# A two-layer hybrid trunk on one core: the last output chunk as a job of its own, new x chunk by chunk, rotary rows swapped by DMA

## The chip, the cores and the metric

The kernel runs as one program on one core of a Trainium2 chip. The metric is the device time of an execution in microseconds (us). The engines are TensorE (PE: matmul; PEld: its weight loads), VectorE (DVE), ScalarE (ACT), GpSimd (POOL) and SyncE (SP), which here only issues DMAs.

## The reference, cut to what matters

Two layers over x of 256 tokens by 1024 channels, all float32. Each layer:

```python
u = _rms_norm(x, pre_mix_norm_w[l])
proj = u @ w_in[l]
qkv_a, z_a, a_a, b_a, cq, ckv, k_rope, gate_logits = _split_cols(proj, PROJ_SIZES)
...
q_b = (_rms_norm(cq, q_a_norm_w[l]) @ w_uq[l]).reshape(b, s, MLA_HEADS, MLA_QK_DIM)
q_b = jnp.concatenate([q_b[..., :MLA_NOPE], _rope(q_b[..., MLA_NOPE:], cos[:, :, None, :], sin[:, :, None, :])], axis=-1)
k_pe = jnp.broadcast_to(_rope(k_rope, cos, sin)[:, :, None, :], (b, s, MLA_HEADS, MLA_ROPE))
y_b = _chunk_causal_attention(q_b, k_b, v_b) @ w_branch_b[l]
h = gates[:, :, 0] * y_a + gates[:, :, 1] * y_b
x = x + _rms_norm(h @ w_out[l], post_mix_norm_w[l])
u = _rms_norm(x, pre_ffn_norm_w[l])
f = jnp.square(jax.nn.relu(u @ w_ff1[l])) @ w_ff2[l]
x = x + _rms_norm(f, post_ffn_norm_w[l])
```

Left out is branch A: short convolution, SiLU, the chunked gated delta rule and a per-head norm, giving y_a. `_rope` turns the two 32-wide halves of a 64-wide rotary part: x1·cos − x2·sin, x2·cos + x1·sin.

## The kernel before

x stays in SBUF, channels on partitions: `xT` is 8 chunks of 128 channels by 256 tokens. Every weight is cut into pieces of 128 x 1024 (152 a layer), fetched by SP in order into a ring of four (`raw`). ScalarE rounds a piece to `whi` (`split_hi`, L973), VectorE makes the rest `wlo` (`split_lo`, L1296). The moving side is split the same way, so each 128x128 weight block costs three products of 256 columns: whi·high (L559), whi·low (L560), wlo·high (L561), in `chunk_products`.

The work is a list of jobs (`JOBS`), each 256 output channels wide into one of three PSUM banks `dense`; a job over 1024 input channels has two pieces and 48 products, a `uq` job one piece, an `ff2` job eight. `schedule()` writes one order (`ORDER`) of jobs and small steps by hand, and every engine walks it with its own part of each step. `splits_wanted` says how far ahead of each step the pieces are split; ScalarE waits there for the piece four back to be released by its products (`steps_done`).

A layer's four borders matter here. "out" (4 jobs) is followed by `ysum`, `post`, `fsplit_x` and then "ff1" (16 jobs); "ff2" (4 jobs) by `ysum`, `post` and the next layer's "lat" jobs (ckv, cq, and one with k_rope) or the end. At such a border ScalarE squares the last job's output (L1095), TensorE adds the squares over channels by products with a matrix of ones (`ysum`, L955: four float32 products of 256 columns), ScalarE takes the inverse root (L984, L986), and `post` on VectorE and GpSimd multiplies `yT` by it (L1618) and adds to `xT` (L1623, and L1733 on GpSimd for chunk pairs 1 and 3). ScalarE then scales and rounds each chunk (`fuh` L1037 or `xh` L1003), VectorE makes the low part (`ful` L1632 or `xl` L1303), and the first job goes chunk by chunk, waiting for the low part.

The "lat" jobs use unnormalised x, so they can run before the norm of x. After the first two of them TensorE adds the squares of x (`norm`, L664), ScalarE takes the root, VectorE and ScalarE make `utmp`, `uh`, `ul`, which the "k" job's first half uses; its second half waits for a piece whose split stands behind these steps.

Rotary: TensorE multiplies by a permutation matrix (`perm`) to swap the 32-row halves of the key (`kr_`, L737) and of two groups of queries (`qrope`, L903); VectorE multiplies by cos and sin and adds. The attention units 0 to 5 run between "gate" jobs (`sc`, `tr`, `pv`; probabilities times values is L945).

Of the kernel before, what the change touches and what calls it, by code (L numbers as in the profile page):

```python
# [23 lines left out]
P = 128  # L24
# [12 lines left out]
PI_BELOW = 3.1415925  # L37
RING = 4
# [17 lines left out]
C_ID, C_UT, C_NEG, C_M1, C_IQ, C_LV, C_ONE, C_PERM, C_AM, C_FREQ = 0, 128, 256, 384, 416, 448, 512, 640, 768, 1024  # L56
# [4 lines left out]
def jobs_of_a_layer():  # L61


    jobs, n = [], 0
    for kind, numbers, pieces in (("lat", range(3), 2), ("k", range(1), 2), ("z", range(1), 2), ("k", range(1, 4), 2),
# [4 lines left out]
                                  ("out", range(4), 2), ("ff1", range(16), 2), ("ff2", range(4), 8)):  # L70
        for i in numbers:
            jobs.append((kind, i, list(range(int(n), max(int(n) + 1, int(n + pieces))))))
            n += pieces
    return jobs, int(n)
# [12 lines left out]
def steps_through(n, job=False):  # L87


    if job:  # L90
        return sum(len(p) for _, _, p in JOBS[:n + 1])
    if n < 0:
        return n + 1
    return sum(len([q for q in p if q <= n]) for _, _, p in JOBS)


NSTEP = steps_through(NJOB - 1, job=True)
# [8 lines left out]
def schedule():  # L106

    o = [("xsplit", 0), ("xsplit", 1), ("sq", 0), ("sq", 1), ("sqsum", 0), ("sq", 2), ("sq", 3), ("sqsum", 1)]
# [113 lines left out]
    for i in range(4):  # L222
        job("out", i)
        if i in (1, 2):
            o.append(("yadd", i - 1))
    o += [("ysum", 0), ("post", 0), ("fsplit_x", 0)]
    for i in range(16):
        o.append(("job", JOB["ff1", i]))
        if i == 0:
            o.append(("squares", 1))  # L230
        if i == 1:
            o.append(("norm", 1))
        flush()
        late.append(("fsplit", i))
    flush()
    for i in range(4):
        job("ff2", i)
        if i in (1, 2):
            o.append(("yadd", 1 + i))
    o += [("ysum", 1), ("post", 1)]  # L240
# [7 lines left out]
def build(nc, x_in, pos_in, w_in, prm_in, cst_in, out):  # L248
    with ExitStack() as ctx:
# [122 lines left out]
        perm = cst[:, C_PERM:C_PERM + P]  # L372
# [48 lines left out]
        x_by_pool, x_by_dve, y_add = (signal("x_by_pool", 4), signal("x_by_dve", 4), signal("y_add", 4))  # L421
# [12 lines left out]
        kr_mm, kr_b, kr_out, ktrans_mm = (signal("kr_mm", 1), signal("kr_b", 2), signal("kr_out", 2), signal("ktrans_mm", 2))  # L434
# [14 lines left out]
        on_hi, on_lo, qr_mm, qr_b = (signal("on_hi", 4), signal("on_lo", 4), signal("qr_mm", 2), signal("qr_b", 4))  # L449
# [4 lines left out]
        h_hi, h_lo, y_sq, y_mm = (signal("h_hi", 4), signal("h_lo", 4), signal("y_sq", 8), signal("y_mm", 2))  # L454
        y_r, y_scaled, f_sq = (signal("y_r", 4), signal("y_scaled", 8), signal("f_sq", 16))
        f_hi, f_lo = (signal("f_hi", 16), signal("f_lo", 16))

# [6 lines left out]
        def products_done(l, j):  # L464

            return l * NSTEP + steps_through(j, job=True) + RING

# [20 lines left out]
        def splits_wanted(l, what, n):  # L488

            if what == "job":  # L490
                ahead = 2 if n == NJOB - 1 else RING
                return min(l * NPIECE + JOBS[n][2][-1] + ahead, DEPTH * NPIECE)
            if what == "half":
                return l * NPIECE + JOBS[n][2][0] + RING
            return l * NPIECE + {("xsplit", 1): 1 + l, ("sq", 0): 2 + l, ("sqsum", 1): 3 + l}.get((what, n), 0)

        splits_at, seen = [], 0
        for l in range(DEPTH):
            for what, n in ORDER:
                goal = max(seen, splits_wanted(l, what, n))  # L500
                splits_at.append(range(seen, goal))
                seen = goal
        assert seen == DEPTH * NPIECE

        def steps_with_splits(l):
            return zip(ORDER, splits_at[l * len(ORDER):(l + 1) * len(ORDER)])
# [3 lines left out]
        def _(sp):  # L510
            def x_part(c):
                sp.dma_start(xT[:, 2 * c:2 * c + 2, :], x_in[:, 2 * c:2 * c + 2, :]).then_inc(s_x[c], 16)

            x_part(0)
            for n in range(DEPTH * NPIECE):
                sp.wait_ge(lo_ready, n + 1)
                sp.dma_start(raw[n % RING][:], w_in[n]).then_inc(loaded[n % RING], 16)
                if n == 0:
                    for c in range(1, 4):
                        x_part(c)  # L520
            for c in range(4):
                pair = slice(2 * c, 2 * c + 2)
                x_pair = x_by_pool if c % 2 else x_by_dve
                sp.wait_ge(x_pair, due(DEPTH, x_pair, 1 + c // 2))
# [5 lines left out]
        def _(pe):  # L530
# [16 lines left out]
            def chunk_products(bank, n, k0, kcount, cols, ahi, alo, first, last, total_k, need=None):  # L547

                h_, l_ = whi[n % RING], wlo[n % RING]
                nch = cols // P  # L550
                for k in range(kcount):
                    if need is not None:
                        need(k0 + k)
                    for c in range(nch):
                        ws = slice(k * cols + c * P, k * cols + (c + 1) * P)
                        o_ = bank[:, c * S:(c + 1) * S]
                        is_first = first and k == 0 and c == 0
                        is_last = last and k == kcount - 1 and c == nch - 1
# [3 lines left out]
                return x_  # L562

            def half(l, j):

                def need(k):
                    if j == JOB["k", 0] and k % 2 == 0:
                        pe.wait_ge(u_lo, due(l, u_lo, k // 2 + 1))
                banks_free(l, j)
                n = JOBS[j][2][0]  # L570
                piece(l, n)
                chunk_products(dense[j % 3], n, 0, 4, 256, uh, ul, True, False, KD, need).then_inc(steps_done, 1)

            def job(l, j):
                kind, i, pieces = JOBS[j]
                bank = dense[j % 3]
                begun = ("half", j) in ORDER
# [1304 lines left out]
```

## Time and profile before

| what | value |
| --- | --- |
| device time, median of 3 runs | 1077.89 us (1075.48 to 1079.14) |
| span of the profiled execution | 1064.2 us |
| median less that span | 13.7 us |
| TensorE busy | 1010.9 us (95%) |
| VectorE, ScalarE, GpSimd busy | 732.4, 557.7, 137.9 us |
| HBM read | 161.25 MB, 153 GB/s over the span |

The page gives the span of one execution, from its first to its last instruction; its device time is not listed apart from the runs', and what lies outside the span is the start and end of the program. Positions below are microseconds from the span's start. Busy time of TensorE includes time at the lower of its two clocks.

### The profile page before, as it was taken

To read this page: it belongs to the slowest core of one execution; us is meant where nothing else is said; L and a number is where in the kernel's file an instruction comes from. 1 tells how busy PE (TensorE), PEld (TensorE's weight loads), DVE (VectorE), ACT (ScalarE), POOL (GpSimd) and SP (SyncE) were. 2 spreads that over 40 slices of the span, in tenths; PEclk is the share of its full clock that TensorE was granted. 3 is DMA by queue.
4 is the path that set the end of the run, shared out by engine and by line. 5 is a ranking of instruction groups with operands and counts; after the bars stand their busy time and mean duration, and the time that the engine had idled before them with its cause. 6 is when DMAs were issued, how large, how long until landed. Compare 5 with 4: busy or idle time off the path is not lost.

```text
span 1064.2 us, 24113 instructions
## 1 busy us (share of the span) xinstructions
PE 1010.9 (95%) x10552; PEld 987.3 (93%) x10552; DVE 732.4 (69%) x982; ACT 557.7 (52%) x786; POOL 137.9 (13%) x109
## 2 busy tenths in 40 slices
PE   5899899999999899999978999999999989999996
PEld 5899889899999899999978998998999979999995
DVE  6886648698566698745388766677875777886453
ACT  6576365755444554443356753767454445444441
POOL 6201000230000322200010000014000013221001
PEclk9999999999999899999989999999999999999998
DMA  7344424334556176666534443334356544766661
GB/s 252 135 141 158 124 82 130 118 106 149 188 180 197 65 224 192 200 196 195 160 119 135 143 142 121 115 106 121 117 166 189 166 153 145 213 197 199 193 185 40
DMA packets 45608, 163.85 MB, mean 154 GB/s; under 512 B 5184, under 2 KB 5440, under 8 KB 45504
## 3 DMA queue, kind: packets, MB, share of 16 engines
q1 hardware_dynamic: 44928, 161.50, 48.2%
q8 instruction: 83, 1.36, 0.5%
q10 hardware_dynamic: 576, 0.82, 0.2%
q14 instruction: 21, 0.17, 0.0%
HBM read 161.25 MB, written 1.05 MB: 153 GB/s over the span
## 4 chain that ended last, share of the span: by engine, by line
PE 91%; DVE 5%; issue 2%; ACT 2%; DMA 1%; POOL 0%; POOLq 0%; SPq 0%; ACTq 0%; DVEq 0%
PE dense L559 25%; PE dense L560 25%; PE dense L561 24%; DVE wlo L1296 1%; PE sides L945 1%; PE sides L799 1%; PE sides L919 1%; PE sides L920 1%; PE sides L791 1%; DVE utmp L1332 1%; PE sides L955 1%; PE sides L759 1%; PE sides L769 1%; PE sides L895 1%; PE sides L718 1%
## 5 line engine op out<-in xcount | busy, mean ns | idle before, releaser
L1296 DVE TENSOR_TENSOR wlo<-raw,whi 128x1024 fp32r<-128x1024 f32 (+1 forms) x304 | 397.9, 1318 | 195.8 <-ACT whi L973 195.5
L973 ACT ACTIVATE whi<-raw 128x1024 fp32r<-128x1024 f32 (+1 forms) x304 | 315.6, 1047 | 225.7 <-PE dense L561 222.0
L559 PE MATMUL dense<-uh,whi 128*128 128x256 f32 x768 | 223.3, 291 | 5.3 <-DVE wlo L1296 5.3
L560 PE MATMUL dense<-ul,whi 128*128 128x256 f32 x768 | 216.3, 282 | 2.6 <-issue 2.6
L561 PE MATMUL dense<-uh,wlo 128*128 128x256 f32 x768 | 216.3, 282 | 0.0
L559 PEld LDWEIGHTS dense<-uh,whi 128*128 128x128 f32 x768 | 147.2, 192 | 7.8 <-DVE wlo L1296 5.7
L559 PE MATMUL dense<-fuh,whi 128*128 128x256 f32 x512 | 144.3, 282 | 9.9 <-DVE ful L1632 9.6
L561 PEld LDWEIGHTS dense<-uh,wlo 128*128 128x128 f32 x768 | 147.2, 192 | 1.6 <-issue 1.6
L560 PEld LDWEIGHTS dense<-ul,whi 128*128 128x128 f32 x768 | 146.7, 191 | 1.5 <-issue 1.3
L560 PE MATMUL dense<-ful,whi 128*128 128x256 f32 x512 | 143.5, 280 | 0.0
L561 PE MATMUL dense<-fuh,wlo 128*128 128x256 f32 x512 | 143.5, 280 | 0.0
L559 PE MATMUL dense<-fh,whi 128*128 128x256 f32 x512 | 141.3, 276 | 0.0
L560 PE MATMUL dense<-fl,whi 128*128 128x256 f32 x512 | 141.3, 276 | 0.0
L561 PE MATMUL dense<-fh,wlo 128*128 128x256 f32 x512 | 141.3, 276 | 0.0
L559 PEld LDWEIGHTS dense<-fuh,whi 128*128 128x128 f32 x512 | 98.3, 192 | 11.1 <-issue 10.3
L560 PEld LDWEIGHTS dense<-ful,whi 128*128 128x128 f32 x512 | 98.2, 192 | 0.1
L561 PEld LDWEIGHTS dense<-fuh,wlo 128*128 128x128 f32 x512 | 98.1, 192 | 0.0
L560 PEld LDWEIGHTS dense<-fl,whi 128*128 128x128 f32 x512 | 96.1, 188 | 0.0
L559 PEld LDWEIGHTS dense<-fh,whi 128*128 128x128 f32 x512 | 96.1, 188 | 0.0
L561 PEld LDWEIGHTS dense<-fh,wlo 128*128 128x128 f32 x512 | 96.1, 188 | 0.0
L1727 POOL TENSOR_TENSOR fr<-fr 128x512 f32<-128x512 f32 x32 | 46.5, 1453 | 119.3 <-DVE fr L1604 119.3
L1697 POOL TENSOR_TENSOR sq<-sq,sq 128x512 f32<-128x512 f32 x8 | 10.4, 1296 | 353.0 <-ACT sq L1095 353.0
(289 smaller groups left out, 1923.2 us busy)
## 6 DMA issues: line engine op xcount, KB each, us to landing
raw<-weights SPq DMA_DIRECT2D x304, 512.0 KB, 3.7
xT<-x_t SPq DMA_DIRECT2D x4, 256.0 KB, 5.7
out_t<-xT SPq DMA_DIRECT2D x4, 256.0 KB, 2.3
cst<-consts ACTq DMA_DIRECT2D x1, 512.0 KB, 6.5
prm_all<-params ACTq DMA_DIRECT2D x1, 150.0 KB, 4.0
pos_i<-pos ACTq DMA_DIRECT2D x1, 128.0 KB, 5.5
cst<-consts ACTq DMA_DIRECT2D x1, 6.0 KB, 5.8
```

Of the source, the lines that this page charges most:

```text
L559: mm(o_, h_[:, ws], ahi[:, k0 + k, :], start=is_first, stop=False, skip_group_check=True)
L560: mm(o_, h_[:, ws], alo[:, k0 + k, :], start=False, stop=False, skip_group_check=True)
L561: x_ = mm(o_, l_[:, ws], ahi[:, k0 + k, :], start=False, stop=is_last, skip_group_check=True)
L718: r = mm(side[KS_BANK[i // 2]][:, c:c + 1], k_squares[i][:, e * S + t * P:e * S + (t + 1) * P], ones[:, 0:1], start=True, stop=True)
L759: r = mm(side[KK_BANK[n]][:, e * P:(e + 1) * P], kT[:, h, ts_], kT[:, h, ts_], start=True, stop=True)
L769: r = mm(side[QK_BANK[n]][:, e * P:(e + 1) * P], kT[:, h, ts_], qT[:, h, ts_], start=True, stop=True)
L791: r = mm(side[e][rows, 16 * g:16 * (g + 1)], LT[rows, g, e, rows], evens(Xq[rows, e, g, :], SIZES[lv]), start=True, stop=True)
L799: r = mm(side[e][rows, 16 * g:16 * (g + 1)], XTq[rows, e, g, :], PBq[rows, e, g, 0:16], start=True, stop=True)
L895: mm(side[2 + i % 2][:], ones, sq[i % 2][:], start=True, stop=True).then_inc(on_mm, 1)
L973: return A(o_, i_, ACT.Copy)
L1296: TT(wlo[s][:, 0:w], raw[s][:, 0:w], f32(whi[s][:, 0:w]), ALU.subtract).then_inc(lo_ready, 1)
L1727: G(fr[i % 4][:], fr[i % 4][:], fr[i % 4][:], ALU.mult).then_inc(f_sq, 1)
```

## The change

1. **Last chunk.** "out" and "ff2" become five jobs: three of 256 channels, then one each for chunk 6 and chunk 7. For "out" both use the same two pieces (`held`); for "ff2" each has four pieces of its own, eight input chunks deep. `early_sums` adds the squares of chunks 0 to 6 (three float32 products) inside the last job; `ysum` keeps one product.
2. **New x by chunk.** `post` becomes the steps `times`, `add`, `high`, `low` over the groups chunk 0, chunk 1, and pairs (2,3), (4,5), (6,7). VectorE does groups 0 to 2, GpSimd both the multiply and the add of (4,5) and (6,7); at the very end VectorE does (4,5) too.
3. **Interleaved first jobs.** Jobs 0 and 1 of "lat" and of "ff1" run together (`pair_of_jobs`): for each x chunk the eight products with the high part once that is there, then, after the low part, the other four. Their pieces are laid out in turns. `ff1` 2's first half goes ahead of `norm` 1.
4. **Splits.** ScalarE and VectorE get tables of their own; pieces for the next stage are split inside the turn.
5. **Rotary.** The `perm` products are gone. SP copies the swapped rows SBUF to SBUF (`swap_key_rows`, `swap_query_rows`, two DMAs each, of 32 KB and 128 KB each), from its one queue of weight loads. The rotary columns are laid out anew; the key's zeroing and adding takes four memsets and four additions of 32 partitions on VectorE instead of two and two of 64.
6. **Probability product.** The very last of unit 5 is done as two products of 64 output rows.

```diff
-                                  ("out", range(4), 2), ("ff1", range(16), 2), ("ff2", range(4), 8)):
+                                  ("out", range(4), 2), ("ff1", range(16), 2), ("ff2", range(3), 8), ("ff2", (3, 4), 4)):
...
+            if kind in PAIRED and i < 2:
+                mine = [int(n) - i, int(n) - i + 2]
...
+        if kind == "out":
+            jobs.append((kind, 4, mine))
...
+NEW_X = [[0], [1], [2, 3], [4, 5], [6, 7]]
+def by_dve(l, w):
+    return 4 if (l, w) == (DEPTH - 1, 1) else 3
...
+    def turn(w):
+        o.extend([("ysum", w), ("post", w)])
+        step = lambda what, g: o.append((what, 5 * w + g))
+        for g in range(2):
+            for what in ("times", "add", "high"):
+                step(what, g)
+        step("low", 0)
+        step("times", 2)
+        step("low", 1)
+        step("add", 2)
+        step("high", 2)
+        for g in (3, 4):
+            for what in ("times", "add", "high"):
+                step(what, g)
+        for g in (2, 3, 4):
+            step("low", g)
...
+    turn(0)
+    o.append(("squares", 1))
     for i in range(16):
+        if i == 2:
+            half("ff1", 2)
+            o.append(("norm", 1))
+            late.extend([("fsplit", 0), ("fsplit", 1)])
...
+            behind = JOBS[JOB["ff2" if n >= 5 else "out", 4]][2][-1] + RING + 1
+            if engine == "act":
+                if what == "high":
+                    return min(base + behind + {0: 0, 4: 1, 5: 0}.get(n, -1), DEPTH * NPIECE)
+                if l:
+                    return base + {("xsplit", 0): 4, ("xsplit", 2): 5, ("sq", 0): 6}.get((what, n), 0)
+            if engine == "dve" and what == "low":
+                return min(base + behind + {3: 0, 4: 1}.get(n % 5, -1), DEPTH * NPIECE)
+            if l:
+                return base + {("xsplit", 2): 6}.get((what, n), 0)
+            return {("xsplit", 1): 1, ("sq", 0): 2, ("sqsum", 1): 3}.get((what, n), 0)
...
+                if p == JOBS[JOB["kn", 0]][2][0] + 6:
+                    swap_key_rows(l)
+                for i in range(2):
+                    if p == JOBS[JOB["uq", 4 + i]][2][0] + 7:
+                        swap_query_rows(l, i)
...
+            def swap_query_rows(l, i):
+                sp.wait_ge(t_oo, due(l, t_oo, 2))
+                sp.wait_ge(act_evac, l * NACT_EVAC + evacs_through(JOB["uq", 4 + i])[1])
+                rotary = qr[:, 2 * i:2 * i + 2, :].rearrange("p c s -> p (c s)")
+                sp.dma_start(E[i][0:ROPE, :], rotary[ROPE:P]).then_inc(qr_swapped[i], 16)
+                sp.dma_start(E[i][ROPE:P, :], rotary[0:ROPE]).then_inc(qr_swapped[i], 16)
...
+            def pair_of_jobs(l, j):
...
+                for k in range(KD):
+                    h_, e = divmod(k, 4)
+                    places = [slice(e * 256 + c * P, e * 256 + (c + 1) * P) for c in range(2)]
+                    pe.wait_ge(high, due(l, high, k + 1))
+                    for jj in both:
+                        n = JOBS[jj][2][h_]
+                        wh, wl = piece(l, n)
+                        for c, ws in enumerate(places):
+                            o_ = dense[jj % 3][:, c * S:(c + 1) * S]
+                            mm(o_, wh[:, ws], a_[:, k, :], start=(k == 0 and c == 0), stop=False, skip_group_check=True)
+                            mm(o_, wl[:, ws], a_[:, k, :], start=False, stop=False, skip_group_check=True)
+                    pe.wait_ge(low, due(l, low, k + 1))
+                    for jj in both:
+                        wh = whi[JOBS[jj][2][h_] % RING]
+                        for c, ws in enumerate(places):
+                            r = mm(dense[jj % 3][:, c * S:(c + 1) * S], wh[:, ws], b_[:, k, :], start=False,
+                                   stop=(k == KD - 1 and c == 1), skip_group_check=True)
+                        if e == 3:
+                            r.then_inc(steps_done, 1)
...
-            def kr_(l, _):
-                pe.wait_ge(vtrans_out, due(l, vtrans_out, 4))
-                mm(side[4][0:64, 0:S], perm[0:64, 0:64], krx[0:64, :], start=True, stop=True).then_inc(kr_mm, 1)
...
-            def qrope(l, i):
-                mm(side[4][:], perm, qr[:, 2 * i:2 * i + 2, :], start=True, stop=True).then_inc(qr_mm, 1)
...
+                        if n == 5 and h == hs[-1] and kt == qt:
+                            for d in (slice(0, 64), slice(64, P)):
+                                r = mm(o_[d], vt[:, kt, h, d], p_, start=False, stop=True)
...
+            def early_sums(l, w):
+                pe.wait_ge(y_add, due(l, y_add, 2 * w + 2))
+                for e in range(2):
+                    mm(side[1][:, 0:S], ones, sq[0][:, e * S:(e + 1) * S], start=(e == 0), stop=False)
+                pe.wait_ge(y_sq, due(l, y_sq, 5 * w + 4))
+                mm(side[1][:, 0:S], ones, sq[1][:, 0:S], start=False, stop=False)
```

## Rows read from the trace of the kernel before

**Rows 1.** The page, first part: busy time of the engines.
```profile
PE 1010.9 (95%) x10552; PEld 987.3 (93%) x10552; DVE 732.4 (69%) x982; ACT 557.7 (52%) x786; POOL 137.9 (13%) x109
```

**Rows 2.** What TensorE waited for: us in total, times, longest us.
```profile
PE dense L559 <- DVE wlo L1296: 19.2, 5, 11.2
```

**Rows 3.** Timeline of TensorE: start, us, instruction [idle before, who ended it].
```profile
38.01 0.39 PE L559 MATMUL dense<-uh,whi 128*128 128x256 f32 x1 [3.86 <-DVE wlo L1296]
...
349.96 0.55 PE L559 MATMUL dense<-fuh,whi 128*128 128x256 f32 x1 [4.78 <-DVE ful L1632]
```

**Rows 4.** Busy time by window; PEclk 1.00 is 2.4 GHz, 0.50 is 1.2 GHz.
```profile
11.20:14.30 3.10, 3.10 (x14) 3.10 (x15) 3.10 (x6) 3.10 (x7) 2.85 (x4) 1.00 0.99 375
...
350.20:355.40 5.20, 5.20 (x25) 5.20 (x26) 4.80 (x9) 2.09 (x6) 1.45 (x1) 0.50 0.01 3
360.00:529.00 169.00, 168.79 (x1480) 168.38 (x1480) 107.80 (x98) 73.56 (x81) 26.99 (x19) 1.00 0.61 192
```

**Rows 5.** Chain that ended last at layer 1's border out to ff1: start, us.
```profile
343.37 1.83 PE sides L955 x8
...
346.18 0.70 DVE yT L1618
...
364.11 1.74 PE sides L664 x8
```

**Rows 6.** The same chain at the border of the layers, and at the end.
```profile
529.55 1.83 PE sides L955 x8
...
553.23 0.88 PE sides L664 x4
...
1052.42 1.83 PE sides L955 x8
```

**Rows 7.** Timelines of GpSimd and VectorE in the ff1 stage.
```profile
394.36 1.42 POOL L1727 TENSOR_TENSOR fr<-fr 128x512 f32<-128x512 f32 x1 [4.02 <-DVE fr L1604]
394.80 2.06 DVE L1296 TENSOR_TENSOR wlo<-raw,whi 128x1024 fp32r<-128x1024 f32 x1
```

**Rows 8.** Groups by line: x count | busy us, mean ns | idle before.
```profile
L1618 DVE TENSOR_TENSOR yT<-yT,rn 128x512 f32<-128x512 f32 x16 | 10.9, 684 | 4.8 <-ACT rn L986 4.8
...
L973 ACT ACTIVATE whi<-raw 128x1024 fp32r<-128x1024 f32 (+1 forms) x304 | 315.6, 1047 | 225.7 <-PE dense L561 222.0
```

**Rows 9.** Timeline of ScalarE: squares of 512 and of 256 columns.
```profile
343.40 0.60 ACT L1095 ACTIVATE sq<-dense 128x512 f32<-128x512 f32 x1 [1.71 <-PE dense L561]
...
564.37 0.36 ACT L1075 ACTIVATE sq_q<-dense 128x256 f32<-128x256 f32 x1
```

**Rows 10.** The chain, layer 1: rotary key, rotary queries, probabilities times values.
```profile
184.28 0.57 PE sides L737 x2
...
204.57 0.86 PE sides L903 x2
...
274.63 0.89 PE sides L945 x8
```

**Rows 11.** DMA issues (KB each, us to landing), and the first use of the rotary key.
```profile
out_t<-xT SPq DMA_DIRECT2D x4, 256.0 KB, 2.3
cst<-consts ACTq DMA_DIRECT2D x1, 6.0 KB, 5.8
...
L920 PE MATMUL sides<-krz,qr x64: 275/328/380, 218.1 to 779.1; 128*128 128x128 f32 x32, 128*128 128x256 f32 x32
```

**Rows 12.** The start: VectorE's second split, the norm's root in both layers, TensorE.
```profile
14.33 1.22 DVE L1296 TENSOR_TENSOR wlo<-raw,whi 128x1024 fp32r<-128x1024 f32 x1
...
25.15 0.48 ACT rn L1021
...
554.13 0.48 ACT rn L1021
...
564.83 0.39 PE L559 MATMUL dense<-uh,whi 128*128 128x256 f32 x1 [1.40 <-DVE wlo L1296]
```

**Rows 13.** Timeline of GpSimd: the last addition.
```profile
1060.20 1.26 POOL L1733 TENSOR_TENSOR xT<-xT,yT 128x512 f32<-128x512 f32 x1 [1.23 <-DVE yT L1618]
```

More of the change, by code:

```diff
@@ L37 @@
 PI_BELOW = 3.1415925
+PAIRED = ("lat", "ff1")
 RING = 4
@@ L82, with steps_of_a_layer, steps_through, steps_of_job @@
 NDVE_EVAC = NJOB - NACT_EVAC
[L87 to L97, printed above, removed]
+def steps_of_a_layer():
+    steps = []
+    for j, (kind, i, pieces) in enumerate(JOBS):
+        if kind in PAIRED and i == 0:
+            steps += [(j + e, JOBS[j + e][2][h_]) for h_ in range(2) for e in range(2)]
+        elif not (kind in PAIRED and i == 1):
+            steps += [(j, n) for n in pieces]
+    return steps
+STEPS = steps_of_a_layer()
+def steps_through(n):
+    return n + 1 if n < 0 else 1 + max(k for k, (_, piece) in enumerate(STEPS) if piece <= n)
+def steps_of_job(j):
+    return 1 + max(k for k, (job, _) in enumerate(STEPS) if job == j)
+NSTEP = len(STEPS)
+def chunks_of(kind, i):
+    return (2 * i, 2 * i + 1) if i < 3 else (i + 3,)
+NEW_X = [[0], [1], [2, 3], [4, 5], [6, 7]]
+def by_dve(l, w):
+    return 4 if (l, w) == (DEPTH - 1, 1) else 3
 def evacs_through(j):
@@ L239, in schedule @@
             o.append(("yadd", 1 + i))
[L240 removed]
+    turn(1)
     return o
@@ L484, in piece_width, with splits_wanted @@
             return KQ * 256 if kind == "uq" else PIECE
-        def splits_wanted(l, what, n):
+        def splits_wanted(l, what, n, engine):
+            base = l * NPIECE
             if what == "job":
-                ahead = 2 if n == NJOB - 1 else RING
-                return min(l * NPIECE + JOBS[n][2][-1] + ahead, DEPTH * NPIECE)
+                kind, i, pieces = JOBS[n]
+                held = kind == "out" and i == 3
+                return min(base + pieces[0 if held else -1] + RING, DEPTH * NPIECE)
@@ L493, in splits_wanted @@
             if what == "half":
[L494 to L506, printed above, removed]
+                return base + JOBS[n][2][0] + RING
@@ L1274, in _ @@
             for l in range(DEPTH):
-                for (what, n), pieces in steps_with_splits(l):
+                for (what, n), pieces in steps_with_splits(l, act_splits):
                     for p_ in pieces:
@@ L1307, in xsplit @@
                 if l == 0:
-                    for e in (range(2), range(2, KD))[part]:
+                    for e in (range(2), range(2, 6), range(6, KD))[part]:
                         x_low(l, e)
@@ L1664, in _ @@
             for l in range(DEPTH):
-                for (what, n), pieces in steps_with_splits(l):
+                for (what, n), pieces in steps_with_splits(l, dve_splits):
                     for p_ in pieces:
@@ L1819, in wide, with in_turns @@
                 pieces.append(blocks(w, 4 * h_, 4, cols))
+        def in_turns(w, first, second):
+            for h_ in range(2):
+                for cols in (first, second):
+                    pieces.append(blocks(w, 4 * h_, 4, cols))
         krope = kr0 + r(ROPE)
```

301 lines of the change are left out of this document (176 added, 125 removed).

## The prediction, made before the changed kernel had run

> **What bounds the kernel now.** I read the page first: TensorE is busy for 1010.9 of the 1064.2 us [rows 1]. Then its waits [rows 2] and its timeline [rows 3]: it hardly waits except at the start, where x or u are renewed, and at the end. So there are two ways to win: fewer products, or shorter borders. The windows show a second cost of a border: after the 4.78 us wait at 349.96 the products run at a granted clock of 0.50, 25 in 5.2 us or 0.21 us each; in the long stretch behind they run at 1.00, 1480 in 169 us, 0.114 us each [rows 4]. Last I read the chain at each border, because it gives a border's whole length, waits and slow clock together: from the sums of squares (343.37) to the end of the first two ff1 jobs (364.11) 20.7 us; between the layers (529.55 to 553.23) 23.7 us; at the end (1052.42 to 1064.2) 11.8 us [rows 5, 6]. The two jobs are 96 products, about 11 us, so each border costs some 10 to 12 us beyond its work.
>
> **Rotary and the halved product.** Over both layers two key products of 0.57 us and four query products of 0.86 us go [rows 10]: 1.14 + 3.44 = 4.6 us. Their lines stand in the chain, so all of it counts. Four probability products take 0.89 us, so one is 0.22 us; cutting it in two adds between 0 (each half takes half) and 0.22 us a layer; I take 0.1, so +0.2. Sum −4.4. The copies are hidden if they land in time. The queries are in SBUF soon after 204.57, where the old product read them, and are first used at 218.1 [rows 10, 11]: 13.5 us. The second group comes one job of 18 products and two sums later, some 4 us, which leaves 9.5, of which VectorE's three steps of 0.68 [rows 8] need 2. No row shows a copy from SBUF to SBUF. Nearest are the output writes of 256 KB, 2.3 us, and a first small load, 5.8 us [rows 11]; both fit. I take 2.3. Ahead of both copies SP waits for an evacuation; behind it stand only weight loads, with four pieces in the ring, at 18 products each (2.1 us) some 8 us, so a stall of 1 to 2 us is covered. VectorE's two more memsets and two more additions per layer, at most four one-chunk operations, 1.7 us, lie under products: it is busy 69% [rows 1]. Without the cover each late microsecond would stop TensorE in both layers.
>
> **A border, first half: up to the inverse root.** Today it takes 2.8 us from the sums to the first multiply (343.37 to 346.18) [rows 5]. The last square shrinks from 0.60 to 0.36 us [rows 9], and one product of ones, 0.43 us (a quarter of the 1.74 at 364.11), stands behind it instead of two: 2.15 us. But the three early sums now stand in the stream of products: +1.3 us, where before two of the four ran under the square. So this half is a loss of 0.6 us at each of four borders; it pays only through one-chunk multiplies.
>
> **A border, second half: the port.** In the ff1 stage a wlo took 2.06 us beside a GpSimd operation (1.42, which itself first waits for VectorE), against 1.22 at 14.33 [rows 7, 12]. So each GpSimd operation holds VectorE up by about 0.85 us, and the change has four at a border for two. The Trainium skill ("SBUF — State Buffer", "SBUF: two separate sides") says the two engines' shared port pair is an exclusive lock, held for the whole instruction; by it each hold would be GpSimd's whole 1.3 us [rows 13], four times 0.45 or 1.8 us more a border; the trace agrees that there is a hold, and shows it at 0.84.
>
> *out to ff1.* A VectorE operation takes 0.68 us for 512 columns and 1.22 for 1024 [rows 8, 12], so for the 256 of one chunk I take 0.42. After the root it does two multiplies, two additions and two low parts of one chunk (2.5), then multiply and addition of a pair (1.3), beside four holds (3.4): 7.2 us. ScalarE's high part of chunk 2 adds 0.5. The first two chunks' 24 products lie inside; 72 are left, at 0.115 us 8.3. Sum 2.15 + 1.3 + 7.2 + 0.5 + 8.3 = 19.4 against 20.7. For the clock I add 0.5: 0 if the shorter waits keep it up, 1.5 if it falls and some 15 products run at 0.21 [rows 4]: −0.8, twice −1.6. Bounds for the pair: −7 with no holds, +4 with holds of 1.3 and a low clock.
>
> *Between the layers.* The second norm needs VectorE's list finished: after the root twelve one-chunk operations (5.0), a pair twice (1.3), three splits (1.15 each, 3.4), three sums of squares (2.0), four holds (3.4), plus 2.5 waiting for ScalarE and for the fourth chunk's products to free the ring. 17.6 + 2.15 + 1.3 = 21.0 against 23.7: −2.7. Bounds −6 and 0.
>
> **The start is a border too, and it gets worse.** The pair needs pieces 0 and 1 at its first chunk. Piece 1's wlo begins at 14.33 and ends at 15.55 [rows 12]; nothing in the diff makes that sooner. Now TensorE fills that time with piece 0, from 11.2 us on [rows 2]; then it does four products and stops. The remaining 92 take 10.5 us at full clock: 26.1. Today's first products run at the slow pace, 14 in 3.1 us, though that column shows 1.00 [rows 4]; these will too, after a longer idle: 20 of them at 0.1 us more, +2, so 28.1 against 24.25 (the root at 25.15 [rows 12] less the 0.9 seen between 553.23 and 554.13): +3.9. Further, both jobs now end together, so before the root ScalarE does two squares and a split between (0.6 + 1.05 + 0.6) [rows 8, 9], 2.3 us where the sums of squares of x take 0.9: 1.3 us more. Against that, GpSimd works on the angle tables during this stretch: root to k's second half is 12.9 us (25.15 to 38.01) in layer 1 and 10.7 (554.13 to 564.83) in layer 2 [rows 3, 12]; shifted later, I give back 2.2. Sum +3.0. Bounds +1 and +5.
>
> **The end.** VectorE: four one-chunk operations (1.7), four of a pair (2.7), two holds (1.7): 6.1, with 2.15 and 1.3 9.5 us to the last addition, where today GpSimd ends at 1061.46, 9.0 us after 1052.42 [rows 6, 13]. Two writes then go out back to back: between 0 and the 2.3 us of one landing [rows 11], I take 0.4. Sum +0.9. Bounds −0.5 and +1.5.
>
> **Sum.** −4.4 − 1.6 − 2.7 + 3.0 + 0.9 = −4.8 us on the span of 1064.2: 1059.4. The median of the runs stands 13.7 above that span, and I leave that alone: 1077.9 − 4.8 = 1073.1 us.
>
> **The rivals.**
> - *Faster than that (24%):* the borders gain what they are laid out for. For it: 10 to 12 us of each border are not products, and the first eight products no longer wait for a low part. Against it: the port. If GpSimd's operations hold VectorE up half as long, each border gains 1.7 more and the start loses 1 less: −4.8 − 6.8 − 1.0, about 1065.5.
> - *The borders cancel the rotary gain (19%):* if the port is held longer (1.2 us a hold) and the granted clock falls in ff1, the two ff1 borders give nothing back and the layer border 1: −4.4 + 0 − 1 + 4 + 1.2, about 1077.7.
> - *Slower (13%), the port alone:* if GpSimd's two-step groups win the port each time VectorE's addition waits for its multiply, chunk 0 is new only after two holds, and the chain by chunk has become a chain by GpSimd operation. The price is four holds of 1.3 us [rows 13] a border, 1.8 us more at each of four, plus 1.5 of slow clock at two: −4.8 + 7.2 + 3 = +5.4, 1083. It decides from about 1.2 us more a border than I count. Against it: wlo at 394.80 was held 0.84 us, not 1.3. The page of the Trainium skill named above states the longer hold.
> - *The copies are late (4%):* if the second query copy takes over 8 us, the scores wait. At 12 us it costs 4 a layer: 1081.
>
> **How the numbers follow.** The likeliest case, 40%, is 1073.1; its own range is 1070 to 1076.5. A measurement of this kernel can tell 0.3%, 3.2 us, from no change, so faster means below 1074.7. That takes the first rival (24%) and three quarters of the likeliest (30%) and a little of the second: 0.55. Same (1074.7 to 1081.1): a quarter of the likeliest (10%), nearly all of the second (18%) and the milder of the slower ones (3%): 0.31. Slower: 0.14. The range 1065 to 1080 leaves out the far half of the fastest and most of the slower rival.
>
> **What would show it.** Right: no rows L737 and L903; TensorE's chain from early sums to the end of the first pair 0.5 to 1.5 us shorter at ff1 and 2 to 3.5 at the layers' border; VectorE's one-chunk addition taking over 1 us beside GpSimd; a new wait of some 3.5 us at the start between the fourth and fifth dense product, ended by wlo; the norm's root in layer 1 at 28 to 31 instead of 25.15; the last addition by VectorE. Wrong: a wait ahead of L920 (copies), or products on the second chunk starting within 5 us of the root (no port), or a first pair held at 0.50 clock for more than 4 us.

## The result and the profile after

The changed kernel takes 1081.27 us (median of 20 runs, 1074.32 to 1090.03), the kernel before, beside it on the same chips, 1073.54 us (20 runs, 1066.20 to 1082.18). The ratio is 1.0091, 95% interval 1.0071 to 1.0112: slower by 0.9%, some 9.8 us (the two medians lie 7.7 us apart), where I had forecast 4.8 us less. The ratios here and below go by the fast executions; left out by them are, among others, one of d_best at 1688.88 us and one of d_ropes at 1518.16. The profiled execution of the changed kernel has a span of 1083.9 us and a device time of 1085.66. So only 1.8 us lie outside the span; the 13.7 us that I left between span and median were for the greater part spread between executions. The two profiled spans are 19.7 us apart, two to two and a half times the distance of the runs, and one pair of profiles must not be read as if it were the median.

The page, first part, changed kernel. TensorE's busy time rose by 10.2 us with eight instructions fewer [rows 1]:

```profile
PE 1021.1 (94%) x10544; PEld 997.4 (92%) x10544; DVE 737.2 (68%) x992; ACT 558.5 (52%) x790; POOL 148.3 (14%) x115
```

What TensorE waited for (us in total, times, longest), changed kernel:

```profile
PE dense L680 <- ACT fuh L1168: 7.3, 2, 3.6
...
PE dense L659 <- DVE wlo L1429: 4.7, 4, 2.6
PE sides L1063 <- DVE E L1695: 4.3, 2, 2.2
PE dense L680 <- DVE wlo L1429: 3.1, 1, 3.1
PE dense L686 <- DVE ful L1783: 2.9, 2, 1.4
```

L680 to L686 are the paired jobs, L659 to L661 the other dense products (L559 to L561 before). The wait of 3.1 us at the fifth product is the one that I had announced. At each ff1 border 3.6 and 1.4 stand for the 4.78 of [rows 3]. The third row answers to nothing before: TensorE stops 2.2 us a layer ahead of the transposes of the first probabilities.

**Rotary.** The chain of the changed kernel from the second query group's issue to those transposes (start, us):

```profile
205.17 0.52 SPq L606
205.72 4.20 DMA E<-qr
209.95 0.69 DVE E L1587
...
211.96 1.70 DVE oT L1670
213.66 0.87 DVE wlo L1429
214.53 1.69 DVE E L1587
...
228.69 0.70 DVE E L1695
229.44 0.86 PE sides L1063 x4
```

and its DMA issues (KB each, us to landing):

```profile
E<-qr SPq DMA_DIRECT2D x8, 128.0 KB, 4.4
...
krb<-krx SPq DMA_DIRECT2D x4, 32.0 KB, 3.1
```

The first copy lands at 209.9, and VectorE, which stood waiting for it (3.18 us idle by its timeline), starts the rotary step there; the same step began at 205.79 before. TensorE does not need the queries until 217.8. But VectorE walks one written list: the norm of branch A (`oT`), three splits and the first softmax stand behind that step, each 3 to 5 us later than before (1.05 of it was there ahead of the stage), and the gaps down to 228.69 take up only about 1 us of that. The lateness comes out at the softmax. How long the stage is can be read between two marks on TensorE, the first products of L991 (L851 before) and the first probabilities times values, L1081 (L945). The kernel before, then the changed one:

```profile
160.79 1.95 PE L851 MATMUL sides<-vtok,XT 128*128 128x128 f32 x16
...
234.76 1.05 PE L945 MATMUL sides<-PT,vt 128*128 128x128 f32 x8
```

```profile
161.84 1.39 PE L991 MATMUL sides<-vtok,XT 128*128 128x128 f32 x11
...
238.80 1.05 PE L1081 MATMUL sides<-PT,vt 128*128 128x128 f32 x8
```

73.97 against 76.96 us: 3.0 longer, though three perm products (2.3 us) are gone. Layer 2 says the same, 73.96 against 76.90.

The wait of 2.16 us is only a part of that; the other is the clock behind it. The transposes and the eight products of the next scores take 3.7 us in the changed kernel (229.44 to 233.15) and 2.0 us before (227.14 to 229.11), 1.7 us more. The same stretch in the changed kernel and in d_ropes (an experiment below, with a wait of 2.31 us at the same place), columns as under "The pace":

```profile
229.40:233.00 3.60, 3.56 (x11) 0.55 0.06 9
```

```profile
230.40:234.00 3.60, 3.53 (x24) 1.00 0.04 6
```

In d_ropes the clock stayed up and they took 2.0 us (230.47 to 232.50). The layer of a_whole in which it stayed up has 75.69 us between the two marks, the one in which it fell 77.55. So a wait of this length did not always bring the clock down here; where it did, wait and slow clock together cost 3.9 us for 2.16 of wait.

**The port.** Timeline of VectorE and GpSimd behind the root at the out to ff1 border, changed kernel:

```profile
348.72 0.43 DVE L1761 TENSOR_TENSOR yT<-yT,rn 128x256 f32<-128x256 f32 x1 [1.15 <-ACT rn L1116]
348.76 1.51 POOL L1877 TENSOR_TENSOR yT<-yT,rn 128x512 f32<-128x512 f32 x1 [6.99 <-ACT rn L1116]
349.18 1.37 DVE L1770 TENSOR_TENSOR xT<-xT,yT 128x256 f32<-128x256 f32 x1
350.35 1.33 POOL L1886 TENSOR_TENSOR xT<-xT,yT 128x512 f32<-128x512 f32 x1
350.47 1.48 DVE L1761 TENSOR_TENSOR yT<-yT,rn 128x256 f32<-128x256 f32 x1
...
351.99 1.38 DVE L1770 TENSOR_TENSOR xT<-xT,yT 128x256 f32<-128x256 f32 x1
...
353.30 1.48 DVE L1783 SCALAR_TENSOR_TENSOR ful<-xT,prm_all,fuh 128x256 fp32r<-128x256 f32 x1
```

One-chunk operations take 0.42 or 0.48 us alone. Each of the four behind the first takes 1.37 to 1.48: four holds of 0.95 to 1.06 us, all on the chain from the root to chunk 1. GpSimd's four operations stand back to back from the root on, and each goes beside one of VectorE's. Four holds were in the forecast as in the slower rival; their size lies between the two (0.85 and 1.3), and chunk 0 is new after one hold, not after two as the rival had it. Each of the four held operations ends 0.27 to 0.29 us after the end of GpSimd's operation beside it: the hold is what was left of that one when VectorE's began, 0.12 to 0.42 us behind it. The page "SBUF — State Buffer" of the Trainium skill ("SBUF: two separate sides") calls the shared port pair an exclusive lock held for the whole instruction; the trace agrees, as far as GpSimd's times can be trusted.

**The pace.** Windows of TensorE in long stretches of dense products; columns are window, length, busy (count), granted clock, DMA share, GB/s. The first window lies in `ya`/`yb`, the second in ff1. Kernel before, then changed kernel:

```profile
285.00:315.00 30.00, 30.00 (x257) 1.00 0.60 185
380.00:420.00 40.00, 40.00 (x355) 1.00 0.68 209
```

```profile
285.00:315.00 30.00, 30.00 (x267) 1.00 0.69 206
380.00:420.00 40.00, 40.00 (x342) 1.00 0.67 202
```

At the same granted clock of 1.00 there are two spacings: 30/267 and 40/355 us a product, and 30/257 and 40/342. A window also counts the products that only reach into it, so these quotients are a little low; from start to start the timelines give 0.1133 and 0.1178 us. The change swapped them: the 564 products of `ya`, `yb` (the outputs of the two branches) and `out` got 2.5 us a layer shorter, the 1392 of the ff1 and ff2 stretch 6.3 us a layer longer. I had read 0.114 as the price of a product and left it alone.

### The profile page after: what moved, and what is told of

Its sections match the earlier page's. It is cut to its first block, busy times and chain, and to the rows that moved or that the text cites. A ratio compares the mean times of both kernels' runs of the same rounds, so it can differ in the third digit from the quotient of the medians.

```text
span 1083.9 us, 24184 instructions
## 1 busy us (share of the span) xinstructions
PE 1021.1 (94%) x10544; PEld 997.4 (92%) x10544; DVE 737.2 (68%) x992; ACT 558.5 (52%) x790; POOL 148.3 (14%) x115
## 3 DMA queue, kind: packets, MB, share of 16 engines
HBM read 161.18 MB, written 1.05 MB: 150 GB/s over the span
## 4 chain that ended last, share of the span: by engine, by line
PE 84%; DVE 9%; issue 3%; ACT 2%; DMA 1%; SPq 0%; ACTq 0%; DVEq 0%
PE dense L659 23%; PE dense L660 22%; PE dense L661 22%; DVE wlo L1429 2%; PE dense L686 2%; PE dense L680 1%; PE dense L681 1%; DVE oT L1670 1%; PE sides L939 1%; PE sides L1081 1%; PE sides L931 1%; ACT whi L1103 1%; DVE yT L1761 1%; DMA E<-qr 1%; PE sides L1051 1%
## 5 line engine op out<-in xcount | busy, mean ns | idle before, releaser
L1429 DVE TENSOR_TENSOR wlo<-raw,whi 128x1024 fp32r<-128x1024 f32 (+1 forms) x304 | 393.3, 1302 | 214.8 <-ACT whi L1103 214.5
L659 PE MATMUL dense<-uh,whi 128*128 128x256 f32 x768 | 222.5, 290 | 4.3 <-DVE wlo L1429 4.3
L661 PE MATMUL dense<-uh,wlo 128*128 128x256 f32 x768 | 215.0, 280 | 0.0
L659 PEld LDWEIGHTS dense<-uh,whi 128*128 128x128 f32 x768 | 146.4, 191 | 6.9 <-DVE wlo L1429 4.9
L661 PEld LDWEIGHTS dense<-uh,wlo 128*128 128x128 f32 x768 | 145.7, 190 | 0.2 <-issue 0.2
L659 PE MATMUL dense<-fh,whi 128*128 128x256 f32 x512 | 144.2, 282 | 0.0
L660 PE MATMUL dense<-fl,whi 128*128 128x256 f32 x512 | 143.8, 281 | 0.0
L661 PE MATMUL dense<-fh,wlo 128*128 128x256 f32 x512 | 143.8, 281 | 0.0
L659 PE MATMUL dense<-fuh,whi 128*128 128x256 f32 x448 | 126.3, 282 | 0.4 <-DVE wlo L1429 0.4
L660 PE MATMUL dense<-ful,whi 128*128 128x256 f32 x448 | 125.8, 281 | 0.0
L661 PE MATMUL dense<-fuh,wlo 128*128 128x256 f32 x448 | 125.8, 281 | 0.0
L659 PEld LDWEIGHTS dense<-fh,whi 128*128 128x128 f32 x512 | 98.2, 192 | 0.1
L661 PEld LDWEIGHTS dense<-fh,wlo 128*128 128x128 f32 x512 | 96.1, 188 | 0.0
L659 PEld LDWEIGHTS dense<-fuh,whi 128*128 128x128 f32 x448 | 85.9, 192 | 0.8 <-issue 0.8
L660 PEld LDWEIGHTS dense<-ful,whi 128*128 128x128 f32 x448 | 84.2, 188 | 0.1
L661 PEld LDWEIGHTS dense<-fuh,wlo 128*128 128x128 f32 x448 | 84.1, 188 | 0.0
```

Of the source, the lines that this page charges most:

```text
L659: mm(o_, h_[:, ws], ahi[:, k0 + k, :], start=is_first, stop=False, skip_group_check=True)
L660: mm(o_, h_[:, ws], alo[:, k0 + k, :], start=False, stop=False, skip_group_check=True)
L661: x_ = mm(o_, l_[:, ws], ahi[:, k0 + k, :], start=False, stop=is_last, skip_group_check=True)
L1429: TT(wlo[s][:, 0:w], raw[s][:, 0:w], f32(whi[s][:, 0:w]), ALU.subtract).then_inc(lo_ready, 1)
```

## The experiments

All of these kernels compute the whole reference. Ratios are to the kernel before, run beside them on the same chip; 0.01 is 10.7 us. Line numbers are each kernel's own.

**Can one small product turn the pace?** a_sum5 and b_sum5 are the changed kernel and the one before with the last norm product ahead of the stretch split by columns; a_whole takes the halved probability product out of the change, b_half puts it alone into the kernel before.

```diff
# a_sum5, b_sum5
-                    r = mm(side[0][:, 0:S], ones, q_[:, c, :], ...)
+                    if w and c == 5:
+                        mm(side[0][:, 0:P], ones, q_[:, c, 0:P], start=False, stop=False, ...)
+                        r = mm(side[0][:, P:S], ones, q_[:, c, P:S], start=False, stop=True, ...)
...
# b_half (a_whole: the reverse)
+                        if n == 5 and h == hs[-1] and kt == qt:
+                            for d in (slice(0, 64), slice(64, P)):
+                                r = mm(o_[d], vt[:, kt, h, d], p_, start=False, stop=True)
...
```

> The changed kernel, with the last of the four norm products ahead of ff1's job 2 (L808) done as two of 128 columns instead of one of 256; nothing else. Pace theory: the products of a long stretch start either 0.113 or 0.118 us apart at the same full clock, and which of the two is settled by the small products between two stretches; one small product more turns it. Then the 1392 products behind that sum, which take 0.118 us each in the changed kernel, take 0.113: 6.3 us less a layer, some 12 us less in all, and the kernel is about as fast as before or faster (1068 to 1072). Rival, borders: the 7 us a layer were lost to VectorE and GpSimd at the borders; one product more changes the time by under 1 us and the windows behind it show 0.118 as before.

> The kernel before, with the last of the four norm products (L664) in two of 128 columns. Pace theory: the 1440 products behind it turn from 0.113 to 0.118 us, 6.5 us more a layer, some 13 us more in all. Rival: the same time within 0.5 us.

> The changed kernel with the last probability product whole again, as before the change. Pace theory: the 564 products of ya, yb and out, 0.113 us apart in the changed kernel, go back to 0.118 (2.5 us more a layer); if the pace is only handed on, the ff stage behind turns as well, to 0.113 (6.3 us less a layer), together 7 to 8 us less. Rival, borders: the same time within 0.5 us, the half product being worth 0.1.

> The kernel before, with only the last probability product halved. Pace theory: ya, yb and out turn from 0.118 to 0.113 us (2.5 us less a layer); the 1440 products of ff1 and ff2 turn from 0.113 to 0.118 if the pace is handed on (6.5 us more a layer), together about 8 us more; if it is not handed on, 5 us less. Rival: the same time within 0.5 us.

Measured: a_sum5 1.0101 (1.0054 to 1.0149) and b_sum5 0.9979 (0.9952 to 1.0006), and neither turned a stretch: my rule "one small product more turns it" fell. b_half gives 0.9925 (0.9892 to 0.9958), 8 us less, a_whole 1.0130 (1.0075 to 1.0186), 4 us above the changed kernel but with overlapping intervals. The window of b_half's profile that answers to the first one above:

```profile
285.00:315.00 30.00, 30.00 (x267) 1.00 0.62 186
```

So the halved product, which I priced at 0.1 us a layer of loss, wins by itself; of the six parts only this one and the rotary were tried alone. Its stretch accounts for 5 of the 8 us. The profile of a_whole does not mirror this cleanly: its `ya`/`yb`/`out` stretch has the short spacing in layer 1 and the long one in layer 2, and its ff stretches, long in the changed kernel, are short in both layers, though its median is no better.

**Rotary alone, and where VectorE waits.** b_rot is the kernel before with part 5 only. The next kernels move VectorE's two rotary steps in the written list.

```diff
# a_late (on the change), b_hrl (kernel before + halved product + copies)
-        if i >= 4:
-            late.append(("qrope", i - 4))
+        if n in (1, 2):
+            late.append(("qrope", n - 1))
# d_ropes (on a_dve below)
+        if n == 1:
+            late.extend([("qrope", 0), ("qrope", 1)])
```

> The kernel before with only part 5 of the change: rotary rows swapped by SP's copies, no perm products. My prediction's step: 4.6 us less over both layers, the copies hidden. Theory from the trace of after: the first query copy lands at 209.6, VectorE stands still for 3.2 us waiting for it (209.95), everything behind it in VectorE's list (norm of the branch, splits, the first softmax) is 3 us late, and the first transposes wait 2.2 us more: from the vtok products to the probability products 2.9 us a layer longer than before instead of 2.2 shorter, so 4 to 6 us slower in all. If instead the loss belongs to other parts of the change, this kernel is 4 us faster than before.

> The changed kernel with VectorE's two rotary steps (qrope) each one uq job later in the written order, behind the branch's norm steps; copies and everything else as in the change. Theory: VectorE does not stand still for the first copy, the wait for the softmax (2.2 us a layer ahead of the first transposes) goes, 2 to 3 us less a layer, 4 to 6 in all. Rival: VectorE's list is simply too full there (memsets, additions and held operations), and the order changes nothing: same within 1 us.

> The kernel before with the halved probability product, the rotary by copies, and VectorE's rotary steps one uq job later. If the copies are hidden this way, it has the 4.6 us of the perm products on top of what the halved product alone gave (ratio 0.9925): about 0.988 to 0.989. If the copies still cost, it is slower than the halved product alone.

> The kernel with the new x all on VectorE (a_dve), and both rotary steps of VectorE behind the first of the branch's norm steps and its split, ahead of the second: late enough for the first copy, early enough for the scores, where putting each one job later made the scores wait 2.16 us for the second. Theory: neither the wait ahead of the scores nor the one ahead of the transposes, so vtok to the first probabilities times values takes 71 to 73 us against 77; 3 to 5 us a layer less than a_dve's. Rival: VectorE's list is too full in any order, and about 2 us of wait stay at one of the two places.

b_rot: 1.0024 (0.9994 to 1.0054). The 0.9957 that my 4.6 us less would have been is outside. Its trace (of one of its longer executions, 1079.68 us) has the wait ahead of the transposes in both layers (2.37 and 2.36 us). a_late: 1.0106 (1.0078 to 1.0134), no gain: that wait went and this one came in its place, since the scores need both groups:

```profile
217.70 0.46 PE L1051 MATMUL sides<-kn,qn 128*128 128x128 f32 x2 [2.16 <-DVE qr L1590]
```

b_hrl: 1.0004 (0.9976 to 1.0031), with the same wait; the copies ate the 8 us that the halved product had brought. d_ropes: 0.9971 (0.9933 to 1.0010), 4 us under its own base a_dve, the intervals overlapping; the wait ahead of the scores is gone, the other is not:

```profile
230.47 0.66 PE L1063 MATMUL sides<-cst,E 128*128 128x128 f32 x4 [2.31 <-DVE E L1695]
```

Its rival holds for the wait: in three orders some 2.2 us come out at one place or the other. But the stage takes 74.49 and 74.54 us between the marks, where a_dve has 77.83 and 76.67; the theory had hoped for 71 to 73, and 1.7 of the us gained in each layer are the clock, which fell behind the wait in both layers of a_dve and in neither of d_ropes. Whether the order did that or the moment, two layers of one profile don't show.

**The copies out of the change.** a_perm is the changed kernel with the perm products back (the functions `kr_` and `qrope` and the column layout as before, no `swap_key_rows` and `swap_query_rows`).

> The changed kernel with the rotary done as before: the perm products on TensorE, no copies. Theory: from the vtok products to the first probabilities times values the copies cost 73.2 against 75 to 76.5 us a layer, so this kernel is 2 to 3 us a layer faster than the change, 4 to 6 us in all, though it has 4.6 us more of products. The prediction's step says the opposite, 4.6 us slower.

1.0074 (1.0042 to 1.0106) against 1.0091: 2 us less, which the intervals don't separate. The marks of the rotary stage, a_perm:

```profile
163.31 1.95 PE L974 MATMUL sides<-vtok,XT 128*128 128x128 f32 x16
...
237.28 0.94 PE L1072 MATMUL sides<-PT,vt 128*128 128x128 f32 x7
```

73.97 us again, exactly the kernel before, with no wait at either place. The copies were put in or taken out, with little else, in four pairs of kernels. By the ratios they cost 2.6 us (b_rot over the kernel before), 1.8 (the changed kernel over a_perm), 8.5 (b_hrl over b_half) and 5.7 (d_start over d_best, below). All four point to a loss where 4.6 was to be won; only the third is clear of the intervals, and the 5.9 us of the profiles lies within their spread.

**GpSimd out of the new x.** a_dve is the changed kernel with `by_dve` at 5, so that VectorE does all five groups.

```diff
-    return 4 if (l, w) == (DEPTH - 1, 1) else 3
+    return 5
```

> The changed kernel with all multiplies and additions of the new x on VectorE, none on GpSimd. Theory of my prediction (the port): each of GpSimd's four operations at a border holds VectorE up by 0.85 us, 3.4 a border, so VectorE doing two pairs more (2.7 us) itself is 0.7 us less a border: about the same time, 0 to 3 us less. Rival: GpSimd works truly beside VectorE and taking it away costs the 2.7 us at each of the four borders, 5 to 10 us more.

1.0011 (0.9979 to 1.0043) against 1.0091: 8.6 us less, by far more than the 0 to 3 that I expected. Groups by line of a_dve, shapes apart (busy, mean ns), and the same of the changed kernel behind them:

```profile
L1770 DVE TENSOR_TENSOR xT<-xT,yT 128x256 f32<-128x256 f32 x8 | 3.4, 424 | 0.3
L1761 DVE TENSOR_TENSOR yT<-yT,rn 128x256 f32<-128x256 f32 x8 | 3.4, 421 | 4.6 <-ACT rn L1116 4.6
```

```profile
L1770 DVE TENSOR_TENSOR xT<-xT,yT 128x256 f32<-128x256 f32 x8 | 10.1, 1258 | 0.3
...
L1761 DVE TENSOR_TENSOR yT<-yT,rn 128x256 f32<-128x256 f32 x8 | 7.6, 953 | 4.6 <-ACT rn L1116 4.6
```

1258 ns against 424 for the same addition. And the order matters beside the sum: a hold early in the list, before chunk 0 and 1 are new, is on the path in full, while the multiplies of the last pairs, which VectorE takes over, lie under the first chunks' products. From the end of the last out product to the norm sums of ff1 the changed kernel takes 23.3 us (346.55 to 369.81), a_dve 20.2 (347.58 to 367.73), each with 24 products more inside than before. This profile of a_dve also has the short spacing in ff1 and ff2, so part of its 8.6 us may be pace. The two ratios come from different rounds, each against the kernel before in its own.

**The start.** d_start adds to a_dve, for the first pair of layer 1 alone, the order of the pieces:

```diff
+                if kind == "lat" and l == 0:
+                    for h_ in range(2):
+                        for jj in both:
+                            n = JOBS[jj][2][h_]
+                            piece(l, n)
+                            chunk_products(dense[jj % 3], n, 4 * h_, 4, 256, a_, b_, h_ == 0, h_ == 1, ...)
+                    return
```

> The kernel with the new x all on VectorE (a_dve), and in layer 1 the first pair of lat jobs in the order of the pieces (job 0's half, job 1's half, twice) instead of by chunk, so that TensorE need not wait for piece 1's low part after four products. Theory of the prediction (the pair costs 3 us at the start by that wait and the slow clock behind it): norm sums at 24 to 25.5 us instead of 27.6 to 29, 2 to 3 us less in all. Rival: the wait moves to the next piece and the time is the same.

0.9941 (0.9902 to 0.9980) against 1.0011, so 7 us less with touching intervals, of which the trace shows 3 to 4 at the start: the wait at the fifth product is gone and the norm sums come at 24.83,

```profile
24.83 1.02 PE L816 MATMUL sides<-usq,cst 128*128 128x256 f32 x4
```

against 29.19 in the changed kernel and 27.93 in a_dve.

**All three undone.** d_best has a_dve, the start and the perm products; of the change it keeps the chunk-wise new x, the pairs at the other borders, the early sums and the halved product.

> The new x all on VectorE, rotary by perm products as before, and the first pair of layer 1 in the order of its pieces. Theory: all three places where the change lost (the port, the copies, the start) are undone, what it gained stays (shorter borders, halved product): 1.5 us less at each ff1 border, 4 at the border of the layers, 5 by the halved product's pace; ratio to before 0.985 to 0.992. Rival: the pace of the long stretches falls the other way and takes it back.

> The best version once more, with its interval. If its first result (ratio 0.9888, interval 0.983 to 0.9946) was not the luck of the pace, the ratio is between 0.985 and 0.993 again.

0.9888 (0.9830 to 0.9946), and again 0.9895 (0.9857 to 0.9933): 11 to 12 us faster than the kernel before and some 21 faster than the change. The rotary stage takes 73.97 us in it, as before; its profile has the short spacing in all four long stretches, so its span (1049.7) flatters it more than its median does. b_half alone has 0.9925 (0.9892 to 0.9958), 8 of these us from one product cut in two; the intervals overlap, so that the other parts bring anything beyond it is not shown.

**Is the pace the program's or the execution's?** The kernel before, the changed one and b_half were profiled a second time, unchanged.

> The kernel before, unchanged, looked at a second time. If the program sets the pace: ya, yb and out at 0.118 us in both layers and ff1 and ff2 at 0.113, as in its first profile. If it differs between executions: another pattern in at least one of the four stretches.

> The changed kernel, unchanged, looked at a second time. If the program sets the pace: ya, yb and out at 0.113, ff1 and ff2 at 0.118 again in both layers. If it differs between executions, another pattern. The waits (3.1 us at the fifth product, 2.16 ahead of the transposes, 3.6 and 1.4 at the ff1 border) are the same in either case.

> The kernel before with the halved probability product only, looked at a second time. If the halving itself sets the pace of ya, yb and out: 0.113 us in both layers again, as in the four other kernels that have it. If not, 0.118 in one or both.

All three repeated `ya`/`yb`/`out`. Over all profiles: with the halved product this stretch had the short spacing in 26 of 26 layers, without it in 2 of 10 (layer 1 of a_whole, layer 2 of b_rot). In ff1 and ff2 the kernel before had the short spacing in 4 of 4 layers and the changed kernel the long one in 4 of 4, but b_half had one of each in its first profile and two short ones in its second, and d_best two short, then one of each. So with the halved product the first stretch's pace is settled; without it, it leans to the long one. The ff stretch's differs between executions of one program. It leans too: short in 9 of 10 layers without the halved product, in 9 of 26 with it. That the halving pushes the ff stretch the other way, as the theory of a pace handed on had it, is therefore possible and not shown.

## Why the prediction was wrong

Term by term, both layers, in the profiled executions. I count from the end of the last product of a stage, and the early sums (1.3 us a border) as part of the border.

| term of the sum | expected | measured | from |
| --- | --- | --- | --- |
| rotary | −4.6 | +5.9 | 73.97 → 76.96, 73.96 → 76.90 |
| halved product | +0.2 | −5.1 | spacing of 564 products a layer |
| out → ff1, two | −1.6 | +4.4 | 20.6 → 21.9 and 19.2 → 22.3, without the 24 moved products |
| layer border | −2.7 | about 0 | 23.5 → 22.1 + 1.3 |
| start | +3.0 | +1 to +2 by L991, +4.1 at 38.01 → 42.12 | 160.79 → 161.84; second profiles 161.44 → 163.49 |
| end | +0.9 | +1.3 | 11.8 → 11.8 + 1.3 |
| spacing in ff1 and ff2 | not in the sum | +12.5 | 1392 products a layer |

The sum is about 20, the distance of the two spans (19.7).

- *"The copies are hidden if they land in time"* failed, and it is the step that turned the sign of the largest term. I measured the copies' time (4.4 us, where I took 2.3) against TensorE's first use, 13.5 us away, and gave the 4% rival a threshold of 8 us. The deadline was VectorE's: its list reached the rotary step 3 us before the copy landed. I had named only SP's queue behind the waits, not VectorE's. And a late microsecond was to stop TensorE for a microsecond; behind the wait of 2.16 us the granted clock was low for 1.7 us more.
- *The halved product, "between 0 and 0.22 a layer"*: only its work was priced. It sets the spacing of the stretch behind it. That this is the cause is shown by b_half (short in four of four layers, where the kernel before has none); by what mechanism stays open.
- *out → ff1*: the mechanism, four holds, was right, and their size (0.85 each) nearly: 4.0 us measured for 3.4. The 0.84 of [rows 7] was one hold, by a split that began 0.44 us behind GpSimd's operation (394.80 and 394.36); at the border VectorE begins 0.12 to 0.42 behind and waits longer. Mis-sized were the rest: the square after a one-chunk output still cost 0.47 us of wait, and I built the pair's products up at 0.115 us with 0.5 for the clock. The windows of that pair in the changed kernel, the first with its second wait inside:

```profile
351.40:354.80 3.40, 2.00 (x8) 0.50 0.00 0
354.90:358.60 3.70, 3.70 (x17) 0.50 0.03 7
```

  25 products at 0.21 us, 2.5 us more than at full clock, as many as in [rows 4]: a wait of 3.6 us in place of 4.8 did not keep the clock up. The prediction's own sign against it, a first pair held at 0.50 for more than 4 us, came. In layer 2 the start distances show 31 such products against 16 before, which is 1.5 of the 3.1 us lost there.
- *Between the layers*: same holds, no gain. With GpSimd out of the borders (d_best) the norm sums of layer 2 come 12.2 us earlier than before (540.89 for 553.07), where those of layer 1 come at the same time (23.84 and 24.09); the first out to ff1 border and the halved product are in that too.
- *The start* was right in mechanism: the 3.5 us wait was 3.13, the root came at 31.07, and from there to k's second half it took 11.05 us where it had been 12.9. In size it was +4.1 at that place for +3.0, and of it only 1 to 2 us are left at L991; what gives the rest back was not looked at. *The end* was right within 0.4.
- *"Slower, the port alone"* (13%) came near in time (5.4 us over the kernel before, for 7.7 to 9.8 measured), and in part by luck. Its four longer holds are there, at 1.0 us and not 1.3, and chunk 0 was new after one hold, not two. It was priced at 10.2 us above the forecast; taking GpSimd out of the borders was worth 8.6, part of which may be pace. It did not decide alone: by the profiles the rotary and the ff spacing cost as much or more.
- *"I leave that alone"*, of the 13.7 us between span and median: the spread of executions, 16 us in 20 runs of either kernel. The spacing of one or two ff stretches, 6 us each, can be a part of it.

The medians are 7.7 us apart, 9.8 by the ratio, and the spans 19.7. What is left open is how much of the ff stretches' 12 us the changed kernel pays on average: its profiles show it in 4 of 4 layers, its median bears out at most a part. The rotary and the border terms stand in both profiles.

## What to carry to other kernels

When a transfer or a wait is put in place of an instruction, its deadline is the moment at which the in-order engine that waits for it would have come by, not the moment at which the bounding engine needs the result; follow that engine's list to the next thing that the bounding engine wants. Work given to GpSimd beside VectorE was paid for here by VectorE operation for operation, so look for a place for it behind the results that a chain waits for. Price a wait of the bounding engine with the clock behind it, not by its length alone. Price a stretch of identical products by the distance from start to start, in two profiles of the same kernel, before trusting any sum of a few microseconds.

## What the runs showed of the hardware

- 128x256 dense products run 0.1133 or 0.1178 us apart at a granted clock of 1.00, over 500 to 1400 products on end; the spacing changed only at interruptions (small products, waits). Splitting a float32 sum ahead of the ff stretch in two did not change it; halving one probability product ahead of `ya` did.
- A VectorE addition of 128x256 took 0.42 us alone and 1.37 beside a GpSimd operation of 1.3 to 1.5 us; four held operations each ended 0.27 to 0.29 us behind GpSimd's.
- Behind a wait of TensorE of 2.16 us the granted clock was 0.55 over the next 3.6 us, and 12 small products took 3.7 us; behind one of 2.31 us in d_ropes it was 1.00, and they took 2.0.
- A copy of 128 KB from SBUF to SBUF landed after 4.4 us and one of 32 KB after 3.1, while an output of 256 KB took 2.1 to 2.3.
